# Two post-norms worked by column chunk, their gate rows made ahead, and 56 products of the identity behind wo2

## The reference, cut to what matters

```python
def rms_norm_2(x, g):
    y = x * rsqrt(mean(x * x, axis=-1, keepdims=True) + EPS)
    return y * g

y  = gated_merge(y_c, y_h, p_gc, p_gh, w_out)             # ends with the product by w_out
x  = x + ga_m * rms_norm_2(y, norm_post_mix)              # "post3" in the kernel
h2 = modulate(rms_norm_2(x, norm_pre_mlp), sh_f, sc_f)    # "norm4": h * (1 + scale) + shift
x  = x + ga_f * rms_norm_2(sq_relu_mlp(h2, mlp_w1, mlp_w2), norm_post_mlp)   # "post4"
return x
```

## Time and profile before

| | |
|---|---|
| time, median of 3 runs | 2971.78 us (2967.68 to 2972.05) |
| profiled execution: its own time, its span | 2973.79 us, 2972.0 us |
| PE busy | 2857.4 us (96% of the span) |
| DVE, ACT, POOL busy | 2014.7 us (68%), 1355.9 us (46%), 146.9 us (5%) |
| DMA | 622.52 MB, mean 209 GB/s |
| mean granted TensorE clock | 0.982 |

### The profile page before, as it was taken

One profiled execution on the slowest core, in us unless ns is written; L12 is line 12 of the kernel. 1 busy time (PEld: TensorE's weight loads), 2 busy tenths in 40 slices (PEclk: granted clock), 3 DMA queues, 4 the chain that ended last, 5 costly groups with the idle time before them and its releaser, 6 DMA issues.

```text
span 2972.0 us, 34985 instructions
## 1 busy us (share of the span) xinstructions
PE 2857.4 (96%) x13258; PEld 2370.4 (80%) x13258; DVE 2014.7 (68%) x2263; ACT 1355.9 (46%) x1633; POOL 146.9 (5%) x103
## 2 busy tenths in 40 slices
PE   7998999999999999999999999989979999999997
PEld 6786787888888887787788888888857888888886
DVE  4665779799789787776686487575557754544554
ACT  4446354444443454555444444653434444344442
POOL 0100001010010100000000000000000001010000
PEclk9999999999999999999999999999989999999998
DMA  7661878987878988555666666405547876665653
GB/s 227 198 195 51 277 255 282 320 266 271 286 258 285 324 287 276 177 184 177 202 184 193 194 188 182 131 1 184 190 144 241 275 220 185 193 189 191 188 188 120
DMA packets 322668, 622.52 MB, mean 209 GB/s; under 512 B 27415, under 2 KB 29591, under 8 KB 320919
## 3 DMA queue, kind: packets, MB, share of 16 engines
q1 hardware_dynamic: 319015, 597.96, 63.1%
q10 hardware_dynamic: 3504, 22.55, 2.0%
HBM read 614.14 MB, written 7.24 MB: 209 GB/s over the span
## 4 chain that ended last, share of the span: by engine, by line
PE 83%; DVE 9%; issue 3%; DMA 3%; ACT 2%; SPq 0%; DVEq 0%; POOL 0%; ACTq 0%; POOLq 0%
PE ps L1281 77%; DVE macc L1930 3%; DVE wlo L1741 2%; DMA raw<-w_in 2%; PE ps L1386 1%; PE ps L1256 1%; ACT whi L648 1%; PE ps L1428 1%; PE ps L1646 1%; DVE tcol L2051 1%; PE ps L1628 1%; PE ps L1608 1%; DMA raw<-w_up 0%; DMA raw<-w_o 0%; PE ps L1357 0%
## 5 line engine op out<-in xcount | busy, mean ns | idle before, releaser
L1741 DVE TENSOR_TENSOR wlo<-raw,whi 128x1024 fp32r<-128x1024 f32 x940 | 1171.9, 1252 | 812.0 <-ACT whi L648 807.5
L648 ACT ACTIVATE whi<-raw 128x1024 fp32r<-128x1024 f32 x940 | 995.8, 1060 | 1312.1 <-PE ps L1281 1222.1
L1281 PE MATMUL ps<-whi,hhi 128*128 128x512 f32 x2064 | 811.7, 393 | 1.7 <-DVE hlo L2057 1.2
L1281 PE MATMUL ps<-whi,hlo 128*128 128x512 f32 x2064 | 804.7, 390 | 0.0
L1281 PE MATMUL ps<-wlo,hhi 128*128 128x512 f32 x2064 | 804.3, 390 | 0.0
L1281 PE MATMUL ps<-whi,xhi 128*128 128x512 f32 x1632 | 649.6, 398 | 21.0 <-DVE wlo L1741 16.4
L1281 PE MATMUL ps<-wlo,xhi 128*128 128x512 f32 x1632 | 642.2, 393 | 0.0
L1281 PE MATMUL ps<-whi,xlo 128*128 128x512 f32 x1632 | 641.8, 393 | 0.0
L1281 PEld LDWEIGHTS ps<-whi,hhi 128*128 128x128 f32 x2064 | 388.2, 188 | 83.4 <-DVE hlo L2057 3.1
L1281 PEld LDWEIGHTS ps<-whi,hlo 128*128 128x128 f32 x2064 | 388.0, 188 | 81.6
L1281 PEld LDWEIGHTS ps<-wlo,hhi 128*128 128x128 f32 x2064 | 388.3, 188 | 79.5 <-issue 1.0
(11 more groups left out here) (280 smaller groups left out, 1548.0 us busy)
## 6 DMA issues: line engine op xcount, KB each, us to landing
raw<-w_in SPq DMA_DIRECT2D x296, 512.0 KB, 4.3
raw<-mlp_w SPq DMA_DIRECT2D x256, 512.0 KB, 3.7
mraw<-w_mod SPq DMA_DIRECT2D x192, 512.0 KB, 6.1
raw<-w_up SPq DMA_DIRECT2D x128, 512.0 KB, 5.1
raw<-w_down SPq DMA_DIRECT2D x128, 512.0 KB, 5.3
raw<-w_o SPq DMA_DIRECT2D x32, 512.0 KB, 5.8
raw<-w_ple_gate SPq DMA_DIRECT2D x32, 512.0 KB, 4.2
raw<-w_out SPq DMA_DIRECT2D x32, 512.0 KB, 4.3
```

The costliest lines, as they stand in the source:

```text
L648: nc.scalar.activation(whi[:, s % NSLOT], raw[:, s % NSLOT], ACT.Copy).then_inc(hi_done, 1)
L1281: ins = nc.tensor.matmul(ps[:, bank(par) + th], a[:, kt, th * P:(th + 1) * P], b[:, (s + u) % NSLOT, k], start=(kt == 0 and m == 0), stop= ...
L1741: nc.vector.tensor_tensor(wlo[:, s % NSLOT], raw[:, s % NSLOT], whi[:, s % NSLOT].bitcast(F32), ALU.subtract)\
```

## The change

Post3 and post4 are worked by column chunk, and norm4's rows are turned inside `mlp2`'s first chunk.

- **Gate rows.** `gate_rows` (16 products in the gap, one copy of 2048 columns) becomes `gate_row(n, k, j)`, four products and one copy of 512 columns, into banks 6 and 7. Those of post3 stand in `pw`, those of post4 in chunks 18 and 19 of `mlp2`.
- **post3.** ACT squares each `wo2` chunk in PSUM with a sum (`psum_squares`), DVE multiplies it by the gate from PSUM into `yrow` (`psum_gain`). After the last chunk DVE adds chunk by chunk to `res` (`post_res`), and ACT squares each chunk of `res` behind it (`res_squares`).
- **Identity products.** PE runs 56 products of the identity by itself into bank 7 behind `wo2`, then waits for norm4's scaled rows.
- **norm4.** Two groups are turned ahead of `mlp2`, the other six inside its first chunk (`mlp2_part`), with a wait for each group's `x_lo`.
- **Modulation.** Its last four column blocks move from chunks 0 to 7 of `mlp2` to chunks 8 to 15; `last_mods` stands in chunk 17.
- **post4.** Squares and gate by chunk inside the last four chunks; SP stores four times 512 KB, each behind its `post_res`.

```diff
-WHOLE = {k: n for n, k in enumerate(k for k in ROOTS if k not in ("post0", "post2", "norm3"))}
+WHOLE = {k: n for n, k in enumerate(("norm0", "norm1", "normc", "post1", "norm2"))}
...
-                    ("mlp1", "sbbb", 16, (4,) * 8), ("mlp1", "sssss", 24, (5,) * 8), ("mlp2", "ssss", 0, (4,) * 8)]
+                    ("mlp1", "sbbb", 16, (4,) * 8), ("mlp1", "sssss", 24, (5,) * 8), ("mlp2", "ssss", 8, (4,) * 8)]
...
+            for c in range(4):
+                cs = slice(c * NCH, (c + 1) * NCH)
+                sp.wait_ge(S["res", "post4"], c + 1)
+                sp.dma_start(rows_of(out[0])[:, :, cs], res[:, :, cs]).then_inc(out_done, 16)
...
+            def gate_row_out(n, j, dst):
+                act.wait_ge(gb_done, 4 * n + j + 1)
+                nc.scalar.activation(dst[:, j * NCH:(j + 1) * NCH], ps[:, 6 + j % 2], ACT.Copy).then_inc(gb_out, 1)
...
-                chunk(p0 + 8 * c, evac_to(yrow, c * NCH, g0 + c), extra=slots(wo_slots, 8 * c))
+                chunk(p0 + 8 * c, lambda c=c, g=g0 + c: psum_squares("post3", c, g), extra=slots(wo_slots, 8 * c))
+            for c in range(4):
+                res_squares("norm4", "post3", ojunk, c)
+            first_row("norm4")
+
+            def post4_squares(c):
+                act.wait_ge(acc_free, plan["mlp2"][1] + len(SEQ) * NSB - 4 + c + 3)
...
+                    ins = nc.scalar.activation(ojunk[:, th], yrow[:, th, c * NCH:(c + 1) * NCH], ACT.Square,
...
+            last = 8 * (len(SEQ) * NSB - 4)
+            mlp("mlp2", 16, False, place({**{g: (lambda g=g: mod_high("norm4", g, xhi)) for g in range(8)},
+                                          **{146 + 4 * j: (lambda j=j: gate_row_out(1, j, gbc4)) for j in range(4)},
+                                          **{last + 8 * c + 10: (lambda c=c: post4_squares(c)) for c in range(3)}}))
+            post4_squares(3)
...
+            def gate_row(n, k, j):
+                pe.wait_ge(mcol_done, k + 1)
...
+                for b in range(4):
+                    kt = 4 * j + b
+                    ins = nc.tensor.matmul(ps[:, 6 + j % 2, b * P:(b + 1) * P], mcol[:, k, kt:kt + 1].to_broadcast([P, P]),
+                                           ident, start=True, stop=True)
+                ins.then_inc(gb_done, 1)
...
+            pw_slots = {2: lambda: o2_turn(0), 3: lambda: o2_turn(1), 5: lambda: o2_turn(2), 6: lambda: o2_turn(3),
+                        8: lambda: gate_row(0, 3, 0), 9: lambda: gate_row(0, 3, 1), 12: lambda: gate_row(0, 3, 2), 13: lambda: gate_row(0, 3, 3)}
...
-            gate_rows(3, plan["mlp2"][1])
-            norm("norm4")
-            pe.wait_ge(x_lo, 24)
-            mlp("mlp2", 16, {})
-            gate_rows(4, plan["end"][1])
+            pe.wait_ge(gb_out, 4)
+            for n in range(56):
+                nc.tensor.matmul(ps[:, 7, 0:P], ident, ident, start=True, stop=True)
+            pe.wait_ge(S["xn", "norm4"], 1)
+            pe.wait_ge(S["xm", "norm4"], 1)
+            norm_turn("norm4", 0, xs)
+            norm_turn("norm4", 1, xs)
+
+            def mlp2_part(u):
+                if u + 2 < 8:
+                    norm_turn("norm4", u + 2, xs)
+                pe.wait_ge(x_lo, 16 + u + 1)
+            mlp("mlp2", 16, place({**{u: (lambda u=u: mlp2_part(u)) for u in range(8)},
+                                   **{144 + 4 * j: (lambda j=j: gate_row(1, 4, j)) for j in range(4)}}))
...
+            for c in range(4):
+                chunk(p0 + 8 * c, lambda c=c, g=g0 + c: psum_gain("post3", c, g), extra=slots(wo_slots, 8 * c))
             dve.wait_ge(reload, 16)
+            for c in range(4):
+                dve.wait_ge(acc_free, g0 + c + 3)
+                post_res("post3", yrow, c)
+            chunk_mean_square("norm4", SQ)
+            dve.wait_ge(S["res", "post3"], 4)
+            scaled_row("norm4", res, xs)
...
+            def post4_gain(c):
+                dve.wait_ge(S["sq", "post4"], c + 1)
+                dve.wait_ge(gb_out, 8)
+                cs = slice(c * NCH, (c + 1) * NCH)
+                nc.vector.tensor_tensor(yrow[:, :, cs], yrow[:, :, cs], gbc4[:, cs].unsqueeze(1).to_broadcast([P, TH, NCH]), ALU.mult)\
+                    .then_inc(S["yg", "post4"], 1)
+            last = 8 * (len(SEQ) * NSB - 4)
+            mlp("mlp2", place({0: lambda: [col4(0), col4(1), low4(0)], **{g: (lambda g=g: [col4(g + 1), low4(g)]) for g in range(1, 7)},
+                               7: lambda: low4(7), 137: last_mods, **{last + 8 * c + 13: (lambda c=c: post4_gain(c)) for c in range(3)}}))
+            chunk_mean_square("post4", SS)
+            post4_gain(3)
+            for c in range(4):
+                dve.wait_ge(S["yg", "post4"], c + 1)
+                post_res("post4", yrow, c)
```

More of the change, by code:

```diff
@@ L407, in build @@
                 S[w, k] = sem(f"{w}_{k}")
-        for k in ("post0", "post2", "norm3"):
+        for k in ("post0", "post2", "norm3", "post3", "norm4", "post4"):
             S["sq", k] = sem(f"sq_{k}")
@@ L411, in build @@
         S["yg", "post2"] = sem("yg_post2")
+        S["yg", "post4"] = sem("yg_post4")
         def pieces(w):
@@ L1229, in _ @@
             for c in range(4):
[L1230 to L1246 removed]
+                chunk(p0 + 8 * c, lambda c=c, g=g0 + c: psum_squares("post3", c, g), extra=slots(wo_slots, 8 * c))
[4 more added lines that the diff above has]
+                act.wait_ge(acc_free, plan["mlp2"][1] + len(SEQ) * NSB - 4 + c + 3)
+                if c:
+                    act.wait_ge(S["sq", "post4"], c)
+                for th in range(TH):
+                    ins = nc.scalar.activation(ojunk[:, th], yrow[:, th, c * NCH:(c + 1) * NCH], ACT.Square,
+                                               accum_out=stat[:, SS + 4 * th + c:SS + 4 * th + c + 1])
+                ins.then_inc(S["sq", "post4"], 1)
+            last = 8 * (len(SEQ) * NSB - 4)
[3 more added lines that the diff above has]
+            post4_squares(3)
         @block.tensor
@@ L2367, in _ @@
             wo_slots = {1: lambda: y_low(4), 2: lambda: y_low(5), 4: lambda: y_low(6), 5: lambda: y_low(7)}
+            p0, g0 = plan["wo2"]
             for c in range(4):
-                chunk(plan["wo2"][0] + 8 * c, extra=slots(wo_slots, 8 * c))
-            def norm_mod(k, src, wait_src, gain, shift):
-                mean_square(k, src, wait_src)
-                dve.wait_ge(rstd_done, RMS[k] + 1)
-                nc.vector.tensor_scalar(xs[:, 1], src[:, 1], stat[:, 9:10], None, ALU.mult).then_inc(S["xs", k], 1)
-                for g in range(KT // 2):
-                    mod_col(k, g, gain, shift)
-                    if g:
-                        mod_low(k, g - 1, xhi, xlo)
-                mod_low(k, KT // 2 - 1, xhi, xlo)
@@ L2389, in _ @@
[L2389 removed]
+                chunk(p0 + 8 * c, lambda c=c, g=g0 + c: psum_gain("post3", c, g), extra=slots(wo_slots, 8 * c))
+            dve.wait_ge(reload, 16)
+            for c in range(4):
[4 more added lines that the diff above has]
+            scaled_row("norm4", res, xs)
+            col4 = lambda g: mod_col("norm4", g, mcol[:, 2], modT[:, 3 * KT:4 * KT, 0])
```

140 lines of the change are left out of this document (49 added, 91 removed).

## The result

The changed kernel took 2949.26 us (median of 5 runs, 2947.59 to 2955.77) where the kernel before took 2970.88 (5 runs, 2966.61 to 2972.05) on the same chip. The ratio estimated from all the runs is 0.9937 with a 95% interval of 0.9921 to 0.9953 (that of the two medians alone would be 0.9927). A second group, five runs of the changed kernel and nine of the one before, gave 0.9936 (0.9921 to 0.9950). So it is 0.6% faster, some 19 us.

The account below looks back on a forecast made before the run. The prediction took PE, busy 96% of the span, as the bound, with gains only in two gaps where it stands. Terms -8.4 - 11.5 + 2.8 + 2.5 + 7.5 - 9.2 = -16.3 gave 2955.5 us, range 2949.5 to 2960.5.

Parts of the forecast that it names:

- up to the transposes: From wo2's end to norm4's first transpose: the chunked post3 chain takes 13.1 us instead of 21.5, -8.4.
- from the transposes to the first piece: Ahead of mlp2: PE waits for one group of turns instead of eight, 3.2 us instead of 14.7, -11.5.
- the first chunk at full clock: mlp2's first chunk, now holding six groups of transposes: 26.7 us instead of 23.9, +2.8.
- Gate rows: Gate-row products moved into pw and mlp2, where PE has no slack: +7.5 us.
- Covered work: Squares and gates inside wo2 and mlp2, and modulation moved to chunks 8 to 15, would cost nothing.
- The tail: Behind the last matmul: 14.2 us instead of 23.4, -9.2 (8.6 to 9.8), with the last store landing after 3.3.
- The clock: mlp2's first piece: granted clock falls to half, +2.5 us, chance 0.48; rival that it stays up, 2953.0, chance 0.32.
- The rival of the late products: Behind wo2: identity products end after the scaled rows are ready, up to 12.7 us more, 2968.2; chance 0.04.
- DVE as the bound: Second pass of mlp2: DVE's sums, products and splits slow each chunk; 2979.5 at 3 us a chunk; chance 0.03.
- a wait in place of the gaps: In the gaps, POOL or a late store takes the gain; post4's part alone lost leaves 2964.7, chance 0.02.
- The level: Whole kernel: terms taken from the profiled 2973.79 us give 2957.5; against the median of 2971.78, 2955.5.

Follow-up runs that it names:

- e3_turns_first: Changed kernel with all eight norm4 turns ahead of mlp2's first chunk again: median 2959.85 us, beside 2951.76 for the changed kernel run again.
- e4_gate_transposes: Changed kernel with gate rows made by transposes of the broadcast column instead of identity products: median 2947.00 us, ratio 0.9914 to the kernel before.
- e6_scale_chunks: Changed kernel with norm4's scaling cut into four column blocks and 50 products for 56: median 2950.67 us, beside 2951.76 for the changed kernel again.
- e9_stores_last: Changed kernel with all four output stores waiting for the last post4 addition: one trace, tail 17.60 us where the changed kernel had 13.55.
- e2_transposes: Changed kernel with 112 identity transposes in place of the 56 products: median 2950.48 us, beside 2951.76 for the changed kernel again.
- e1_no_products: Changed kernel without the 56 identity products: median 2951.06 us; stretch from first o2 turn to end 933.26, beside 931.54 for the changed kernel again.
- e8_no_products_again: Changed kernel without the 56 identity products, a second trace: stretch from first o2 turn to end 933.04 us, beside 931.54 with them.
- e10_late_products: Changed kernel with 10 products, issued after post3's last residual, instead of 56: one trace, stretch from first o2 turn to end 931.46 us.
- e5_gain_first: Changed kernel with post4's last gain ahead of the mean square, into its own buffer: tail 12.64 us where the changed kernel had 13.55; median 2951.70.

## Why the prediction was right, and where it was not

**The two gaps and the new chains.** The steps up to the transposes, from the transposes to the first piece, and the first chunk at full clock were priced at -8.4, -11.5 and +2.8 and measured -8.44, -11.46 and +2.88. They were right because each link of the new chains already stood in the trace, at post0, post2 and x2: the same instructions in the same order on the same engines. In the first chunk the starts of every second piece lie 7.0 apart (2209.90, 2216.91, 2223.91), and the last two pieces take 5.8, as forecast. That the first step came within 0.04 is in part luck: the additions took 5.38 instead of 5.64, the last squares with their sums 2.16 instead of 1.84, and the two cancel. And +2.8 is the right sum of two terms that I didn't see apart, 4.7 for the turns and -1.8 for the clock in the first chunk of before (`e3_turns_first`).

**Gate rows.** Priced at +7.5, measured +7.4. PE has no slack inside the stages, so every pass of the moved products is paid in full, and `e4_gate_transposes` shows it from the other side: half the passes, half the cost.

**Covered work.** Squares, gates and modulation at nothing: right, as PE waits for none of them.

**The tail.** The root beside the gain was 1.61 as the row from SBUF had it. The term was mis-sized by the store: I took 3.3 between the estimate of 2.7 and the bound of 3.9, and it landed in 2.9. That is 0.4 of the 0.64 by which the tail came out lower; the rest is `post_res`, 5.39 instead of the 5.64 that I took.

**The clock: the step that failed.** "I take that it does: **+2.5**" was the wrong choice in both its parts. The fall is possible with this code, as `e6_scale_chunks` shows, but it was seen in one of nine traces where I gave it the larger chance; and it cost 1.6, since it did not take the whole piece. With the fall left out the forecast's own terms give -18.8, against -19.45. I leaned on x2's fall, with some 5 us between matmuls of the big kind, for a stretch of 3.2 behind products, and had no row for that. And x2's fall was itself one execution: in five of the fourteen traces, that of the changed kernel among them, x2's first piece ran at full clock.

**The rival of the late products** needed the clock to fall on them. It didn't: 112 passes in 12.66, and 0.64 to spare. That the products "can keep the clock" was the part of the change that I could least price; it turned out at 1.5 to 1.7 us. **DVE as the bound** and **a wait in place of the gaps** are excluded by the waits of PE, and by the landing of the last store.

**The level.** The terms were laid on a profiled execution of 2973.79 and shifted by 2.0 to the median. The medians of the changed kernel (2949.26 and 2951.76) are 18 to 22 below those of before, around the -19.4 of the stretch. The rest is what wanders ahead of the changed code; a median of three or five runs here carries some 3 us of it. So the first median lies 6.2 below the forecast, of which 3.15 are the terms, 0.9 the median of before, which came out lower with five runs, and the other 2.2 wandering. The second median lies inside the range by that same wandering.

By parts, then: the turns in the chunk are worth 9.1 (`e3_turns_first`), some 2.8 of it by the clock; the products 1.5 to 1.7, by the clock alone; the stores by chunk 4.0 (`e9_stores_last`) of the tail's 9.8; and the gate rows cost 7.4, of which 3.7 need not be paid. The chunked chain up to the transposes, 8.4, and the other 5.8 of the tail are read off the two traces; no run undoes them alone. The parts overlap in the clock and don't add to 19.4.

## What to carry to other kernels

When an edit repeats a pattern that the kernel already has, price it from that pattern's rows: chain by chain, that came within 0.1 us here. But look at the pattern in a second execution where the price hangs on the clock: x2's fall, from one trace, was absent in five of fourteen. When work moves from a gap into a stage that PE bounds, count every pass, and ask for the form with the fewest: a broadcast column turned by a transpose took one pass where a 32-bit product took two. Compare kernels over the stretch that holds the change, between the same events, when runs wander by more than the part in question.

A filler of matmuls needs only to stand right ahead of the work that it warms up for: in the one trace of it, ten did what 56 did. And where a small POOL operation is on the path, don't run a DVE operation with two SBUF inputs beside it.

## What the runs showed of the hardware that was not expected

- TensorE's granted clock stays at full (2.4 GHz) through 12.4 us of transposes alone (`e2_transposes`); in the same stretch left empty it falls to half (1.2 GHz; `e1_no_products`, `e8_no_products_again`), and the first five or six matmuls of the next piece still run at half (0.63 instead of 0.39 us each).
- After 8.35 us of standing still, twenty passes ran at half clock (4.6 us), and the transposes behind them at full clock (`e10_late_products`, one trace).
- The same code gets a clock fall in one execution and none in another: in the first attention (a mean of 1.00 over 220 to 260 us in three traces, 0.87 to 0.91 in eleven), in x2's first piece (nine of fourteen), and in one of nine traces behind the third norm. The three traces without the first fall have the three earliest roots, 1.2 to 8.8 us ahead of the other eleven; that the fall is the whole cause isn't shown.
- Eight groups of transposes with 0.3 to 1.1 us of standing still between them let the clock fall, right behind 12.7 us of products (`e3_turns_first`).
- A 128x2 operation of POOL took 1.61 us beside a DVE operation with two SBUF inputs and 0.70 without one (`e5_gain_first`).
- A store of 512 KB landed 2.8 to 2.9 us after its issue when the four were issued some 1.3 us apart (2939.3 to 2943.3), and up to 5.1 when they were issued within 1.8 us (`e9_stores_last`).
